# VectorE writes low parts one chunk further ahead beside the output gates of an HGRN2 layer

## The chip, the core and the metric

The kernel runs on 1 core of one Trainium2 chip. A time is the device time of one execution in microseconds (us). Three runs of the kernel before took 1814.8, 1816.38 and 1819.74 us; the median is 1816.38. The engines are named as in the profile: PE is TensorE (PEld its loads of weights), DVE is VectorE, ACT is ScalarE, SP is SyncE, which only issues DMAs. GpSimd computes nothing here.

## The reference, cut to what matters

One layer of depth 1 on 256 latent and 256 context tokens, width 2048. The mixer is HGRN2, a gated linear recurrence in two directions with 16 heads of 128 channels:

```
m_lat = split(silu(c) @ w_ada + b_ada, 6)            # shift, scale, gate, twice
a     = rms_norm(h) * (1 + scale) + shift            # latent and context
q, v, g = split(a @ w_in)                            # 2048 columns each
z     = clip(a @ w_f[d]), d = forward, backward
f     = lb + (1 - lb) * sigmoid(z);  k = 1 - f;  q = silu(q)
S_t   = diag(f_t) S_(t-1) + k_t v_t^T;   o_t = S_t^T q_t      # both directions, per head
y     = (rms_norm(o) * silu(g)) @ w_o                # g: the output gates
h     = h + gate1 * y
h     = h + gate2 * swiglu(modulated rms_norm(h));   out = rms_norm(h)
```

All products are in float32 precision.

## The kernel before, in words

**Weights in two parts.** A weight chunk is 128 x 1024 numbers. It lands in one of 7 buffers `raw`. ScalarE rounds it to `whi` (3 buffers, L510, function `hi`), VectorE subtracts that from the raw chunk and writes the rest, the low part, over the raw chunk (`rawlo`, L842, function `lo`). TensorE then computes three products for each tile: high by high, high by low, low by high. So each chunk passes ScalarE, VectorE and TensorE, in that order. `lo` waits for `s_hi` of its own chunk; TensorE waits for `s_lo` at the start of a chunk; `hi` of a chunk waits until TensorE has used up the chunk three before it.

**Positions.** Every engine walks one list, `positions()`, with one weight chunk per position. Chunks 0 to 127 give queries, values and forget gates of eight pairs of heads. Chunks 128 to 159 give the output gates (kind "G"); this text calls them g0 to g31, and their positions too. Then come the output projection, the gate and up projections of the FFN and the down projection.

**Scan steps.** Beside the matmuls of a position every engine works on a list of scan steps (j, n): step j of 14 of head n. Beside the output gates these are the steps of the last four heads, 12 to 15, by `tasks_tail`. On VectorE step 0 makes cumulated gates (L1035 to L1046), 1 and 2 the exponents of seven levels (L986, L987), 3 and 4 multiply the levels (L1005, L1006), 5 the operands of the state (L1057 to L1063), 7 and 9 place scores (L1013, L1017), 8 a state (L1079), 13 the normed output (L1085). Steps 6, 10, 11 and 12 have nothing on VectorE. On ScalarE step 2 is L648, step 3 L651, step 4 L634 to L645, step 7 L655, step 8 L659, step 11 L663, step 12 L668 and L670. On TensorE step 6 turns the operands (L1540) and step 11 sums squares (L1576).

**What VectorE does in a position**, in its order: `lo` of the chunk of the next position; clipping of the gates of the last pair (L950, in g0) and their logs and keys (L961, L963, L970, in g2 to g6); an output gate's product (L1093, in g11, g19 and g27); the scan steps of the list; and then a block of the adaLN weights, multiplied by silu(c) and added up (L934, L937, function `ada`), in g1, g4 to g18 and g20.

**What ScalarE does in a position**: `hi` of the chunk of the next position; exponents and logs of the last pair's gates (L594 to L597, g1 to g4); the SiLU of a unit of output gates with two loads of its table (L679, L681, in g10, g18 and g26); the scan steps; and the sigmoid (L604) that belongs to the logs. Each engine takes its instructions strictly in the program's order.

**Loads.** SyncE fills the seven `raw` buffers in the ring's order, in which weight chunks and adaLN blocks alternate here. A buffer is free again when TensorE has used the chunk (`s_used`) or VectorE has added the block (`s_ac`).

Of the kernel before, what the change touches and what calls it, by code (L numbers as in the profile page):

```python
# [64 lines left out]
def mod_blocks(ck):  # L65

    return list(range(FIRST + 4 * ck, min(FIRST + 4 * ck + 4, 64)))


C_G = C_B + GROUPS * BODY  # L70
C_WO = C_G + 4 * 8
# [15 lines left out]
def tasks_at(p, groups=True):  # L87

    return [(p - s, off) for s, off in head_slots() if 0 <= p - s <= 13]


def tasks_tail(p):

    out = []
    for s, head, stretched in ((-11, HEADS - 4, False), (-3, HEADS - 3, False), (5, HEADS - 2, True), (14, HEADS - 1, True)):
        for j in range(14):
            at = s + (6 * j) // 5 if stretched else s + j
            if at == p:
                out.append((j, head))
    return out  # L100


def positions():


    for g in range(GROUPS):
        for p in range(BODY):
            tasks = [(j, 4 * g + off) for j, off in tasks_at(p) if 4 * g + off >= 0]
            if g == 0 and p < 16:
                yield C_B + p, ("VQ", "Z")[p % 2], 0, p // 2, tasks  # L110
            else:
                yield C_B + g * BODY + p, "Z" if p % 16 >= 8 else "VQ", 2 * g + p // 16, p % 8, tasks
    for p in range(32):
        yield C_G + p, "G", p // 8, p % 8, tasks_tail(p)


def build(nc, x, c, ctx, c_ctx, w_ada, b_ada, norm_mix, norm_ffn, lb_logits, w_in, w_f, o_norm, w_o,
# [13 lines left out]
    with stack:  # L131
        at = {}
# [324 lines left out]
        def low(ck):  # L457

            return rawlo[:, SEQ["w", ck] % RAW, :]
# [15 lines left out]
        def ada_sum(e):  # L475

            return bank[3] if e < 6 else mx
# [361 lines left out]
        def _(dve):  # L839
            def lo(ck):  # L840
                dve.wait_ge(s_hi, ck + 1)
                dve.tensor_tensor(low(ck), raw[:, SEQ["w", ck] % RAW, :], whi[:, ck % SPL, :].bitcast(F32),  # L842
                                  ALU.subtract).then_inc(s_lo, 1)
# [9 lines left out]
            def mod_lo(n):  # L853
                if mod_direct(n):
                    return
                j = SPLIT_MOD.index(n)
                dve.wait_ge(s_mh, j + 1)
                dve.tensor_tensor(dlow[n % MRAW][:, :], dslot[n % MRAW], mhi[j % MHI][:, :].bitcast(F32),
                                  ALU.subtract).then_inc(s_ml, 1)

            def modulation(e):


                dve.wait_ge(s_at, e + 1)
                b = bias[:, 2 * e:2 * e + 2]
                nm = vec[:, R_NMIX + 2 * e:R_NMIX + 2 * e + 2]
                each_b = bass.AP(tensor=b.tensor, offset=b.offset, ap=[list(b.ap[0]), [KD, 2], [1, 2], [0, 2]])
                each_nm = bass.AP(tensor=nm.tensor, offset=nm.offset, ap=[list(nm.ap[0]), [1, 2], [0, 2]])
                turned = mod_bank(e)[:, 0:16].rearrange("p (m k i s) -> p m k i s", m=2, k=2, i=2)
                v = modx[:, 2 * e:2 * e + 2, :, :].rearrange("p k m i -> p m k i")  # L870
                dve.tensor_tensor(v, turned[:, :, :, :, 0], each_b, ALU.add).then_inc(s_md, 1)
                dve.wait_ge(s_md, 3 * e + 1)
                dve.tensor_tensor(v, turned[:, :, :, :, 1], v, ALU.add).then_inc(s_md, 1)
                dve.wait_ge(s_md, 3 * e + 2)
                dve.scalar_tensor_tensor(out=scl[:, 2 * e:2 * e + 2, :], in0=modx[:, 2 * e:2 * e + 2, 1, :], scalar=1.0,
                                         in1=each_nm, op0=ALU.add, op1=ALU.mult).then_inc(s_md, 1)

            def a_lo(k):
                dve.wait_ge(s_ah, k + 1)
                dve.tensor_tensor(alo[:, k, :], xn[:, k, :], ahi[:, k, :].bitcast(F32), ALU.subtract).then_inc(s_al, 1)  # L880

            def x_norm(k):
                dve.tensor_tensor(xn[:, k, :], xT[:, k, :], rstd[:, :], ALU.mult).then_inc(s_xn, 1)
# [58 lines left out]
            def clip_gates(pr):  # L942
                if pr >= 2:
                    dve.wait_ge(s_cum, 2 * pr - 2)
                for i, (d, h) in enumerate(UNITS):
                    if i < 3:
                        dve.wait_ge(s_zd, 3 * pr + i + 1)
                    else:
                        dve.wait_ge(s_used, C_B + 16 * (pr + 1))
                    dve.tensor_scalar(gates[pr % 2][:, h, d, :], z_out(pr, 2 * d + h), -CLIP, CLIP, ALU.max,  # L950
                                      ALU.min).then_inc(s_zc, 1)

            def log_gates(pr, i):

                d, h = UNITS[i]
                b = pr % 2
                n = 4 * pr + i
                G, K = gates[b][:, h, d, :], keyq[b][:, h, 2 * d, :]
                dve.wait_ge(s_ze, 3 * n + 3)
                dve.wait_ge(s_zc, n + 1)  # L960
                dve.tensor_tensor(K, G, zt[:, i % 2, 0, :], ALU.add).then_inc(s_zy, 1)  # L961
                dve.wait_ge(s_zy, 2 * n + 1)
                dve.tensor_tensor(G, zt[:, i % 2, 1, :], zt[:, i % 2, 0, :], ALU.subtract).then_inc(s_zy, 1)  # L963

            def keys(pr, i):
                d, h = UNITS[i]
                K = keyq[pr % 2][:, h, 2 * d, :]
                dve.wait_ge(s_mod, 1)
                dve.wait_ge(s_zk, 4 * pr + i + 1)
                dve.tensor_scalar(K, K, oml[:, 2 * pr + h:2 * pr + h + 1], None, ALU.mult).then_inc(s_k, 1)  # L970

            def scale_queries(pr):
                dve.wait_ge(s_qev, pr + 1)
                Q = keyq[pr % 2][:, :, 1, T:TT]
                dve.tensor_scalar(Q, Q, QSCALE, None, ALU.mult).then_inc(s_qs, 1)
# [112 lines left out]
            def gate_outputs(u):  # L1088
                for i in range(2):
                    dve.wait_ge(s_gev, 2 * u + i + 1)  # L1090
                    dve.wait_ge(s_on, 4 * u + 2 * i + 2)
                    v = oT[:, 4 * u + 2 * i:4 * u + 2 * i + 2, :]
                    dve.tensor_tensor(v, v, zt[:, i, 0, :].rearrange("p (k t) -> p k t", k=2), ALU.mult).then_inc(s_y, 1)  # L1093

            def add_modulation(e):
# [3 lines left out]
                o = 2 * KD + 8 * e  # L1099
                dve.tensor_tensor(v, ada_sum(e)[:, 0:8], bias[:, o:o + 8], ALU.add).then_inc(s_av, 1)  # L1100

            for ck, kind, u, r, tasks in positions():
                if u == 0 and kind == "VQ":
                    for n in mod_blocks(ck):
                        mod_lo(n)
                    if r < 5:
                        x_norm(6 + 2 * r)
                        x_norm(7 + 2 * r)
                if u == 0 and kind == "Z" and r < 7:
                    for n in mod_blocks(ck)[:3]:  # L1110
                        mod_lo(n)
                    modulation(r + 1)
                    a_lo(2 * r + 2)
                    a_lo(2 * r + 3)
                    for n in mod_blocks(ck)[3:]:
                        mod_lo(n)
                lo(ck + 1)
                p = (ck - C_B) % 16
                if p == 0 and C_B + 16 <= ck <= C_G:
                    clip_gates((ck - C_B) // 16 - 1)  # L1120
                if ck == C_B + 16:
                    scale_queries(0)
                if kind == "Z" and r == 1 and u:
                    scale_queries(u)
                if 2 <= p < 7 and C_B + 16 <= ck < C_G + 7:
                    pr = (ck - C_B) // 16 - 1
                    if p <= 5:
                        log_gates(pr, p - 2)
                    if p >= 3:
                        keys(pr, p - 3)  # L1130
                if kind == "G" and r == 3 and u:
                    gate_outputs(u - 1)
                for e in ada_ends(ck - 1):
                    add_modulation(e)
                for j, n in tasks:
                    scan(j, n)
                for i in ada_blocks(ck):
                    ada(i)

# [66 lines left out]
            for u in range(2 * FG):  # L1206
                for r in range(8):
                    ck = C_FF + 8 * u + r
# [451 lines left out]
def ada_blocks(ck):  # L1660
    return [i for i in range(PADA) if ada_chunk(i) == ck]
# [14 lines left out]
def ada_ends(ck):  # L1676

    return [e for e in range(PADA // KD) if ada_chunk(KD * e + KD - 1) + 2 == ck]
# [43 lines left out]
```

## Time and profile before

| what | value |
|---|---|
| median of three runs | 1816.38 us |
| the profiled execution | 1817.04 us |
| its span, first to last instruction | 1815.3 us |
| busy over the span: PE, DVE, ACT | 97%, 71%, 50% |
| mean granted TensorE clock, as a share | 0.994 |
| DMA over the span | 353.84 MB, mean 195 GB/s |

The chain that ended last is PE for 86% and DVE for 9% of the span. Busy shares are means over stages that have different limits; the output gates take only about 140 of the 1815 us, from about 832 to 972 us after the start.

### The profile page before, as it was taken

What the parts mean: (1) busy time and instruction counts of PE and PEld (TensorE: products, weight loads), DVE (VectorE), ACT (ScalarE), POOL (GpSimd) and SP (SyncE); (2) the same over time, 40 slices, a digit from 0 to 9 for tenths busy, and PEclk for the clock granted to TensorE, in tenths of its full rate; (3) what the DMA queues carried; (4) which work ended last, traced back from release to release, by engine and by line L of the source; (5) the groups of instructions that cost most, each with busy time, mean ns of one, the idle gap of its engine ahead of it and who ended that gap; (6) DMA issues with size and microseconds to landing.
All of it is one profiled execution on the core that took longest, in us unless ns stands there. A gap on an engine that the chain in (4) does not pass through costs nothing.

```text
span 1815.3 us, 25245 instructions
## 1 busy us (share of the span) xinstructions
PE 1764.5 (97%) x9791; PEld 1503.9 (83%) x9791; DVE 1284.5 (71%) x1999; ACT 915.4 (50%) x1297; POOL 0.2 (0%) x4
## 2 busy tenths in 40 slices
PE   7999999999999999999889989999999999999997
PEld 3667989898989898988789878888888888888886
DVE  5876979796979796979985575555555555555755
ACT  5776635353645454545455554444444444445544
POOL 0000000000000000000000000000000000000000
PEclk9999999999999999999999999999999999999999
DMA  8987745554444554445657556777767777666553
GB/s 292 300 276 240 220 152 151 153 167 134 152 140 143 153 179 130 151 138 142 216 193 263 186 152 212 229 231 224 227 215 237 222 227 227 218 195 195 190 195 128
DMA packets 203737, 353.84 MB, mean 195 GB/s; under 512 B 17953, under 2 KB 116578, under 8 KB 202594
## 3 DMA queue, kind: packets, MB, share of 16 engines
q1 hardware_dynamic: 203426, 352.18, 61.8%
q8 instruction: 77, 1.26, 0.3%
q14 instruction: 42, 0.34, 0.1%
q10 hardware_dynamic: 192, 0.05, 0.0%
HBM read 350.06 MB, written 2.11 MB: 194 GB/s over the span
## 4 chain that ended last, share of the span: by engine, by line
PE 86%; DVE 9%; issue 2%; ACT 2%; DMA 1%; ACTq 0%; SPq 0%; DVEq 0%
PE bank L1476 9%; PE bank L1478 9%; PE bank L1477 9%; PE bank L1342 7%; PE bank L1343 7%; PE bank L1344 7%; PE bank L1359 3%; PE bank L1360 3%; PE bank L1361 3%; PE bank L1496 3%; PE bank L1497 3%; PE bank L1498 3%; PE score L1558 2%; PE score L1496 1%; PE score L1497 1%
## 5 line engine op out<-in xcount | busy, mean ns | idle before, releaser
L842 DVE TENSOR_TENSOR rawlo<-raw,whi 128x1024 fp32r<-128x1024 f32 x456 | 556.4, 1223 | 378.5 <-ACT whi L510 377.8
L510 ACT ACTIVATE whi<-raw 128x1024 fp32r<-128x1024 f32 x456 | 481.1, 1058 | 596.2 <-PE bank L1478 240.6
L1342 PE MATMUL bank<-ahi,whi 128*128 128x256 f32 (+1 forms) x976 | 333.4, 342 | 10.7 <-DVE rawlo L842 10.5
L1343 PE MATMUL bank<-alo,whi 128*128 128x256 f32 (+1 forms) x976 | 325.8, 334 | 0.0
L1344 PE MATMUL bank<-ahi,rawlo 128*128 128x256 f32 (+1 forms) x976 | 325.7, 334 | 0.0
L1476 PE MATMUL bank<-whi,ahi 128*128 128x512 f32 x704 | 275.9, 392 | 1.8 <-DVE alo L1188 1.8
L1478 PE MATMUL bank<-whi,alo 128*128 128x512 f32 x704 | 274.6, 390 | 0.0
L1477 PE MATMUL bank<-rawlo,ahi 128*128 128x512 f32 x704 | 274.5, 390 | 0.0
L1342 PEld LDWEIGHTS bank<-ahi,whi 128*128 128x128 f32 x976 | 185.4, 190 | 31.7 <-DVE rawlo L842 10.2
L1344 PEld LDWEIGHTS bank<-ahi,rawlo 128*128 128x128 f32 x976 | 185.2, 190 | 18.4
L1343 PEld LDWEIGHTS bank<-alo,whi 128*128 128x128 f32 x976 | 185.5, 190 | 17.3
L1476 PEld LDWEIGHTS bank<-whi,ahi 128*128 128x128 f32 x704 | 132.6, 188 | 29.3 <-issue 2.2
L1478 PEld LDWEIGHTS bank<-whi,alo 128*128 128x128 f32 x704 | 132.5, 188 | 27.8
L1477 PEld LDWEIGHTS bank<-rawlo,ahi 128*128 128x128 f32 x704 | 132.6, 188 | 27.2
L937 DVE SCALAR_TENSOR_TENSOR aacc<-raw,cs,aacc 128x1024 f32<-128x1024 f32 x120 | 153.3, 1277 | 0.5
L1359 PE MATMUL bank<-whi,ahi 128*128 128x256 f32 x512 | 148.1, 289 | 1.2 <-DVE arena L950 1.2
L1361 PE MATMUL bank<-whi,alo 128*128 128x256 f32 x512 | 144.7, 283 | 0.0
L1360 PE MATMUL bank<-rawlo,ahi 128*128 128x256 f32 x512 | 144.7, 283 | 0.0
L1359 PEld LDWEIGHTS bank<-whi,ahi 128*128 128x128 f32 x512 | 98.0, 191 | 4.8 <-DVE rawlo L842 2.4
L1360 PEld LDWEIGHTS bank<-rawlo,ahi 128*128 128x128 f32 x512 | 97.9, 191 | 0.8
L1361 PEld LDWEIGHTS bank<-whi,alo 128*128 128x128 f32 x512 | 97.8, 191 | 0.0
L1496 PE MATMUL bank<-whi,ahi 128*128 128x512 f32 x240 | 93.6, 390 | 1.0 <-DVE rawlo L842 1.0
(233 smaller groups left out, 2487.8 us busy)
## 6 DMA issues: line engine op xcount, KB each, us to landing
raw<-in_w_ada_dram SPq DMA_DIRECT2D x128, 512.0 KB, 4.1
raw<-in_ffn_w_gate_dram SPq DMA_DIRECT2D x88, 512.0 KB, 3.7
raw<-in_ffn_w_up_dram SPq DMA_DIRECT2D x88, 512.0 KB, 3.7
raw<-in_ffn_w_down_dram SPq DMA_DIRECT2D x88, 512.0 KB, 4.5
raw<-in_hg_w_in_dram SPq DMA_DIRECT2D x128, 256.0 KB, 4.0
raw<-in_hg_w_f_dram SPq DMA_DIRECT2D x128, 256.0 KB, 4.0
work<-in_w_ada_dram SPq DMA_DIRECT2D x66, 256.0 KB, 5.2
raw<-in_hg_w_in_dram SPq DMA_DIRECT2D x32, 512.0 KB, 4.8
```

What stands on the lines that cost most here:

```text
L510: act.activation(whi[:, ck % SPL, :], raw[:, q % RAW, :], ACT.Copy).then_inc(s_hi, 1)
L842: dve.tensor_tensor(low(ck), raw[:, SEQ["w", ck] % RAW, :], whi[:, ck % SPL, :].bitcast(F32), ALU.subtract).then_inc(s_lo, 1)
L1342: pe.matmul(dst, w, ah, start=start, stop=False, skip_group_check=True)
L1343: pe.matmul(dst, w, al, start=False, stop=False, skip_group_check=True)
L1344: return pe.matmul(dst, wl, ah, start=False, stop=stop, skip_group_check=True)
L1359: pe.matmul(dst, ahi[:, k, tk], whi[:, s, o], start=st, stop=False, skip_group_check=True)
L1360: pe.matmul(dst, ahi[:, k, tk], low(ck)[:, o], start=False, stop=False, skip_group_check=True)
L1361: last = pe.matmul(dst, alo[:, k, tk], whi[:, s, o], start=False, stop=end, skip_group_check=True)
L1476: pe.matmul(dst, ahi[:, k, tk], whi[:, s, o], start=first, stop=False)
L1477: pe.matmul(dst, ahi[:, k, tk], low(ck)[:, o], start=False, stop=False)
L1478: last = pe.matmul(dst, alo[:, k, tk], whi[:, s, o], start=False, stop=end)
L1496: pe.matmul(dst, ahi[:, slot, tk], whi[:, s, o], start=start, stop=False)
```

## The change

In the position of an output gate chunk whose list of scan steps and adaLN blocks holds two things or more, VectorE writes, behind its first scan step, the low part of the chunk after the next (`lo(ck + 2)`). The next position then leaves its own `lo` out. The rule holds in g0 to g2, g4 to g18 and g20, 19 of the 32 positions. The number of instructions is the same. TensorE's, ScalarE's and SyncE's instructions are the same and in the same order; only VectorE's order changes.

```
+            early = set()
             for ck, kind, u, r, tasks in positions():
...
-                lo(ck + 1)
+                if ck not in early:
+                    lo(ck + 1)
...
-                for j, n in tasks:
+                ahead = kind == "G" and C_G <= ck < C_WO - 1 and len(tasks) + len(ada_blocks(ck)) >= 2
+                for at, (j, n) in enumerate(tasks):
                     scan(j, n)
+                    if ahead and at == 0:
+                        lo(ck + 2)
+                        early.add(ck + 1)
                 for i in ada_blocks(ck):
                     ada(i)
```

VectorE in g1 before. The first row is the low part of g2, the row before last that of g3; between them lie step 4 of head 13 and an adaLN block (L937); the last row begins g2:

```order
L842 TENSOR_TENSOR rawlo<-raw,whi 128x1024
L1005 TENSOR_TENSOR work<-work,arena 128x2x16x8
L1006 TENSOR_TENSOR work<-work,arena 128x2x16x8
L1005 TENSOR_TENSOR work<-work,arena 128x2x32x4
L1006 TENSOR_TENSOR work<-work,arena 128x2x32x4
L1005 TENSOR_TENSOR work<-work,arena 128x2x64x2
L1006 TENSOR_TENSOR work<-work,arena 128x2x64x2
L1005 TENSOR_TENSOR work<-work,arena 128x2x128
L1006 TENSOR_TENSOR work<-work,arena 128x2x128
L937 SCALAR_TENSOR_TENSOR aacc<-raw,cs,aacc 128x1024
L842 TENSOR_TENSOR rawlo<-raw,whi 128x1024
L961 TENSOR_TENSOR arena<-arena,zt 128x512
```

The same position now. The first row is here the low part of g3, since g2's stands in g0 already, ahead of step 3 of head 13:

```order
L842 TENSOR_TENSOR rawlo<-raw,whi 128x1024
L1005 TENSOR_TENSOR work<-work,arena 128x2x16x8
L1006 TENSOR_TENSOR work<-work,arena 128x2x16x8
L1005 TENSOR_TENSOR work<-work,arena 128x2x32x4
L1006 TENSOR_TENSOR work<-work,arena 128x2x32x4
L1005 TENSOR_TENSOR work<-work,arena 128x2x64x2
L1006 TENSOR_TENSOR work<-work,arena 128x2x64x2
L1005 TENSOR_TENSOR work<-work,arena 128x2x128
L1006 TENSOR_TENSOR work<-work,arena 128x2x128
L937 SCALAR_TENSOR_TENSOR aacc<-raw,cs,aacc 128x1024
L961 TENSOR_TENSOR arena<-arena,zt 128x512
L963 TENSOR_TENSOR arena<-zt 128x512
```

The low part of g3 has moved ahead of step 4 of head 13 and of the adaLN block.

VectorE at the end of g5 and in g6, the difference (minus: before, plus: now). The first row is g5's adaLN block. The low part is that of g7 where it is taken away and that of g8 where it is put in; L1013 and L1017 are step 9 of head 13, the L986 and L987 behind them step 1 of head 14:

```order
 L937 SCALAR_TENSOR_TENSOR aacc<-raw,cs,aacc 128x1024
-L842 TENSOR_TENSOR rawlo<-raw,whi 128x1024
-L970 TENSOR_SCALAR arena<-arena,oml 128x512
-L1013 TENSOR_TENSOR work<-score,ident 128x128
-L1017 COPY_PREDICATED work<-masks,score 128x128 x7
+L970 TENSOR_SCALAR arena<-arena,oml 128x512
+L1013 TENSOR_TENSOR work<-score,ident 128x128
+L1017 COPY_PREDICATED work<-masks,score 128x128 x7
+L842 TENSOR_TENSOR rawlo<-raw,whi 128x1024
 L986 TENSOR_TENSOR work<-work 128x2x2x64
 L987 TENSOR_TENSOR work<-work 128x2x2x64
```

In g7 the list is step 10 of head 13, step 2 of head 14 and a block; step 10 has nothing on VectorE, so the low part of g9 stands right behind g6's block, where that of g8 stood, and the rows there read alike.

VectorE from the end of g18 to g20, the difference. The low part taken away is that of g19; L1093 is the product of an output gate in g19, then follow the low part of g21, L1085 (step 13 of head 14) and L1057 (step 5 of head 15) in g20:

```order
 L1006 TENSOR_TENSOR work<-work,arena 128x2x128
 L937 SCALAR_TENSOR_TENSOR aacc<-raw,cs,aacc 128x1024
-L842 TENSOR_TENSOR rawlo<-raw,whi 128x1024
 L1093 TENSOR_TENSOR work<-work,zt 128x512 x2
 L842 TENSOR_TENSOR rawlo<-raw,whi 128x1024
 L1085 SCALAR_TENSOR_TENSOR work<-ob,vec,rstd 128x256
+L842 TENSOR_TENSOR rawlo<-raw,whi 128x1024
 L1057 TENSOR_TENSOR work<-work,arena 128x384
```

The low part taken away there is that of g20, which now stands in g18; the one put in is that of g22, ahead of step 5 of head 15. That of g21 keeps its place.

## Rows read from the trace of the kernel before

**Rows 1.** The page: busy us, share and instructions of each engine
```profile
PE 1764.5 (97%) x9791; PEld 1503.9 (83%) x9791; DVE 1284.5 (71%) x1999; ACT 915.4 (50%) x1297; POOL 0.2 (0%) x4
```

**Rows 2.** Windows: length, busy us per engine (instructions), granted clock, DMA share, GB/s
```profile
830.00:925.00 95.00, 78.32 (x613) 75.28 (x612) 93.07 (x178) 55.35 (x87) 0.00 (x0) 0.98 0.62 202
941.00:1040.00 99.00, 99.00 (x572) 87.44 (x572) 55.52 (x73) 52.28 (x72) 0.00 (x0) 1.00 0.65 218
```

**Rows 3.** Waits of PE and DVE, 830 to 925: total us, times, longest
```profile
PE bank L1342 <- DVE rawlo L842: 10.5, 7, 3.7
DVE rawlo L842 <- ACT whi L510: 0.5, 1, 0.5
```

**Rows 4.** Timeline of DVE, g0 to g2: start, us, idle before in brackets
```profile
834.72 0.41 DVE L1005 TENSOR_TENSOR work<-work,arena 128x256 f32<-128x256 f32 x1
...
836.72 1.22 DVE L842 TENSOR_TENSOR rawlo<-raw,whi 128x1024 fp32r<-128x1024 f32 x1
...
840.55 1.27 DVE L937 SCALAR_TENSOR_TENSOR aacc<-raw,cs,aacc 128x1024 f32<-128x1024 f32 x1
841.74 1.21 DVE L842 TENSOR_TENSOR rawlo<-raw,whi 128x1024 fp32r<-128x1024 f32 x1
842.88 0.68 DVE L961 TENSOR_TENSOR arena<-arena,zt 128x512 f32<-128x512 f32 x1
...
844.20 0.48 DVE L1085 SCALAR_TENSOR_TENSOR work<-ob,vec,rstd 128x256 f32<-128x256 f32 x1
```

**Rows 5.** Timeline of ACT, the end of g1, and g2
```profile
839.88 1.04 ACT L510 ACTIVATE whi<-raw 128x1024 fp32r<-128x1024 f32 x1
...
843.59 0.63 ACT L604 ACTIVATE arena<-arena 128x512 f32<-128x512 f32 x1 [0.87 <-DVE arena L961]
844.13 1.04 ACT L510 ACTIVATE whi<-raw 128x1024 fp32r<-128x1024 f32 x1
```

**Rows 6.** Timeline of DVE, behind step 1 and step 2 of head 14
```profile
869.66 1.28 DVE L937 SCALAR_TENSOR_TENSOR aacc<-raw,cs,aacc 128x1024 f32<-128x1024 f32 x1
...
874.68 1.27 DVE L937 SCALAR_TENSOR_TENSOR aacc<-raw,cs,aacc 128x1024 f32<-128x1024 f32 x1
875.87 1.22 DVE L842 TENSOR_TENSOR rawlo<-raw,whi 128x1024 fp32r<-128x1024 f32 x1
```

**Rows 7.** Timeline of ACT, g7 and g8
```profile
869.78 1.49 ACT L648 ACTIVATE work<-work 128x1536 f32<-128x1536 f32 x1 [7.45 <-DVE work L987]
871.17 1.04 ACT L510 ACTIVATE whi<-raw 128x1024 fp32r<-128x1024 f32 x1
...
876.61 1.04 ACT L510 ACTIVATE whi<-raw 128x1024 fp32r<-128x1024 f32 x1
```

**Rows 8.** Timeline of DVE, g16 to g20
```profile
917.06 1.28 DVE L937 SCALAR_TENSOR_TENSOR aacc<-raw,cs,aacc 128x1024 f32<-128x1024 f32 x1
...
927.75 1.23 DVE L842 TENSOR_TENSOR rawlo<-raw,whi 128x1024 fp32r<-128x1024 f32 x1
```

**Rows 9.** Timeline of ACT, g17 and g18
```profile
918.99 1.04 ACT L510 ACTIVATE whi<-raw 128x1024 fp32r<-128x1024 f32 x1
920.05 1.28 ACT L679 ACT_TABLE_LOAD   x1
...
926.67 1.05 ACT L510 ACTIVATE whi<-raw 128x1024 fp32r<-128x1024 f32 x1
```

**Rows 10.** Timeline of DVE in g20 (step 5 of head 15), and of PE
```profile
932.63 0.75 DVE L1063 TENSOR_TENSOR work<-work,arena 128x256 f32<-128x256 f32 x2
933.44 0.55 PE L1540 MATMUL mx<-ident,work 128*128 128x128 f32 x3
```

**Rows 11.** Windows around the one fall of the clock in this stage
```profile
910.00:915.00 5.00, 1.32 (x11) 1.12 (x11) 4.98 (x10) 2.43 (x2) 0.00 (x0) 1.00 0.88 295
915.00:920.00 5.00, 5.00 (x32) 5.00 (x31) 5.00 (x11) 2.83 (x2) 0.00 (x0) 0.66 0.26 95
```

## The prediction

> **What bounds the kernel now.** I read the page's busy table first. Over the whole span TensorE is busy 97% and VectorE 71% [rows 1], so a change of VectorE's order is worth something only in a stretch where VectorE is the late one. The windows show where that is. From 830 to 925 us VectorE is busy 93.07 of 95 us and TensorE only 78.32; from 941 to 1040 us TensorE is busy all 99.00 us and VectorE 55.52 [rows 2]. The change acts in g0 to g20, from about 832 to 935 us, so nearly all of it lies in the first kind of stretch. The waits of that stretch come next: TensorE waits 10.5 us in seven pauses for low parts, while VectorE waits 0.5 us in all for a high part [rows 3]. VectorE's order of work is then the path. TensorE's pauses there are a result of VectorE's length, not a store of time that an order can give back, and any new pause of VectorE is paid in full. Last I laid the timelines of VectorE and ScalarE beside each other, position by position.
>
> **What the change does to VectorE's length.** It removes nothing and adds nothing: 19 subtractions go forward past work that stays. Their own cost is the same. What is new is their wait. The low part of the chunk after the next needs that chunk's high part, which ScalarE makes only behind all scan steps and gate work of the present position. Before, VectorE asked for a high part that ScalarE had written a position earlier, and so it waited 0.5 us in 95 [rows 3]. Now it asks about one position earlier. Behind the waiting subtraction stand the rest of the scan steps and the adaLN block, in order, and SyncE's next load waits for the block's buffer. So I compare for each moved low part when VectorE gets to it and when the high part is there. Prices from start to start: a low part 1.14 us (842.88 - 841.74), three levels' multiplications 2.00 (836.72 - 834.72), four levels' 2.69 (840.55 - 837.86, where 837.86 = 836.72 + 1.14), the block 1.20 (841.74 - 840.55 = 1.19), the logs of a gate 1.32 (844.20 - 842.88) [rows 4].
>
> Low part of g3, in g1. Step 12 leaves nothing on VectorE, so the subtraction stands right behind step 3 of head 13. VectorE gets there at 834.72 + 1.14 + 2.00 = 837.86. ScalarE's high part begins at 839.88 and ends at 840.92 [rows 5]; ScalarE is busy with gate exponents and step 4, none of which comes sooner. Pause 3.06.
>
> Low part of g4, in g2. VectorE goes on at 840.92 and gets there at + 1.14 + 2.69 + 1.20 + 1.32 + 0.40 (L1085) = 847.67. ScalarE's sigmoid starts 0.71 behind L961 (843.59 - 842.88) and the high part is done 1.58 later (844.13 + 1.04 - 843.59) [rows 4, 5]. L961 starts at 845.95, so it is there at 848.24. Pause 0.57.
>
> Low parts of g5 to g7 have the same logs and sigmoids. That of g5 keeps its place and its pause of 0.5; for g7 I take 0.2 new.
>
> Low part of g9, in g7. Step 10 leaves nothing on VectorE. It gets there at 869.66 + 1.20 = 870.86 (there g8's subtraction stood) [rows 6]. ScalarE has the long exponentials of step 2 first, which start when VectorE's levels end, and then the high part from 871.17 to 872.21 [rows 7]. Pause 1.35.
>
> Low part of g10, in g8. The same with step 3: VectorE at 875.87 [rows 6], the high part from 876.61 to 877.65 [rows 7]. Pause 1.78.
>
> g10 to g16: from here ScalarE has little, since VectorE is late already and most positions give it one short step. I count 0.
>
> Low part of g19, in g17. Reckoned from the end of step 2 of head 15 at 917.06 [rows 8], VectorE now has g18's low part and the block first: 917.06 + 1.14 + 1.20 = 919.40. The high part runs from 918.99 to 920.03 [rows 9]. Pause 0.63.
>
> Low part of g20, in g18. Step 11 leaves nothing on VectorE. It gets there at 920.03 + 1.14 + 2.00 + 1.20 = 924.37. ScalarE has two table loads around the SiLU from 920.05, steps 11 and 4, and then the high part from 926.67 to 927.72 [rows 9]. Before, VectorE took that chunk at 927.75, just behind it [rows 8]. Pause 3.35.
>
> The pauses add to 3.06 + 0.57 + 0.2 + 1.35 + 1.78 + 0.63 + 3.35 = 10.9 us. Low parts g21 and later that keep their place are late by as much.
>
> The handover. In g20 the subtraction of g22 now stands ahead of step 5 of head 15, another 1.14 us. TensorE turns the result of that step (L1540) at 933.44, and VectorE's L1063 ends at 932.63 + 0.75 = 933.38 [rows 10]: TensorE has 0.06 us of room. So TensorE gets past this point 10.9 + 1.14 - 0.06 = 12.0 us later. Behind it TensorE is busy without a gap [rows 2] and nothing is given back. The whole delay goes to the end.
>
> Sum, against the profiled execution's 1817.04 us: 1817.04 + 12.0 = 1829.0. That execution is 0.66 above the median of 1816.38, so against the median 1828.4.
>
> **A rule weighed.** VectorE starts its instructions in order in every row I read, and the pause in front of a subtraction holds back what is behind it. The Trainium skill, page "TensorE: Matmul & The Clock Gate", section "Architectural detail: the array is 16× 32×32, not 1× 128×128", says that ScalarE and VectorE have strict first-in first-out queues while TensorE may pull weight loads forward. By that rule the pauses cost what I reckon; if the waiting subtraction could be passed by the multiplications behind it, the 10.9 would be near 0. No row before shows a pass, so the trace agrees.
>
> **Bounds of the unknown.** Each pause is the distance of two rows, right if ScalarE's chain keeps its place against VectorE's. If TensorE, late with steps 10 and 11, holds ScalarE up (L663 needs its sums), they grow; the largest pause of TensorE so far is 3.7 us [rows 3], and I allow one such, + 4. If the smaller pauses (0.57, 0.2, 0.63) vanish and those of g9 and g10 halve, 3.0 goes. Nothing here can be below zero but the handover, where the gain rival sits. Own range of the forecast: 1825 to 1833.
>
> **Rivals.**
>
> Nothing moves. VectorE's sum is unchanged and the pauses are taken up because VectorE would have waited anyway. For it: the low part alone needs no new work. Against it: VectorE has only 95 - 93.07 = 1.9 us free in the stretch [rows 2]. Time 1816.4.
>
> Only the first pause stays. If ScalarE, which is busy only 55.35 of 95 us [rows 2], runs further ahead than I think once VectorE is 3 us late, later pauses shrink: 3.06 + 0.57 + 1.14 = 4.8. Time 1821.2. Against it: ScalarE's steps 2 and 3 start on VectorE's own ends, so they shift with VectorE [rows 7].
>
> Faster. TensorE's seven waits for low parts vanish since each low part is there a position sooner; 10.5 us at most, 1805.9. It decides if high parts are ready when asked for. It needs VectorE to have room, which it has not; a partial version gives the one large wait of 3.7 [rows 3], at 1812.7.
>
> More than reckoned: the clock. TensorE was busy 1.32 us of 910 to 915, and in the next 5 us its granted clock was 0.66 on the mean, that is some 3.4 us at the lower of its levels, 1.2 GHz; it cost nothing since TensorE then waited anyway [rows 11]. With longer pauses of TensorE there will be two to four such falls. One that meets TensorE where it is the late engine costs half of 3.4, 1.7 us, and then delays high parts through used chunks. With two of them and the 4 us above it is 1828.4 + 7 = 1835. The Trainium skill, the same page, section "What's actually happening", has it that the throttled clock is the default and activity releases it. By that rule too the longer pauses bring more falls, and the trace agrees with the one it shows.
>
> **How the numbers follow.** Forecast 0.73, more than reckoned 0.06, only the first pause 0.09, nothing 0.08, faster 0.04. A measurement here can tell about 0.3%, 5.4 us, from no change. Slower by more: 0.73 + 0.06 and about half of the 0.09, 0.84. Within: the other half and most of nothing, 0.12. Faster: 0.04. The range 1821.5 to 1833 takes in the forecast's own range and reaches down to the case of one pause.
>
> **What the changed profile would show.** VectorE's waits for L510 in the stretch of the output gates rise from 0.5 to about 11 us, with pauses near 3 us in front of the low parts of g3 and g20, and 1.3 and 1.8 in front of g9 and g10. TensorE waits longer for L1063 of head 15, and its unbroken stretch begins some 12 us later. Everything behind it, from the output projection on, is the old timeline shifted by 12. Wrong would be a VectorE without pauses there (then high parts come earlier than I read), or an unbroken stretch of TensorE that starts as early as before although VectorE paused.

## The result, and the profile after

The changed kernel took 1832.21 us (median of 4 runs, 1828.53 to 1835.57), the kernel before beside it 1817.1 us (median of 4, 1814.8 to 1819.74). The ratio is 1.0082, with a 95% interval of 1.007 to 1.0094: slower by about 15 us. The profiled execution took 1828.53 us, with a span of 1826.7 us, 11.5 us above the one of before.

The page of after, busy us and share of each engine (answers to [rows 1]):

```profile
PE 1765.0 (97%) x9791; PEld 1505.2 (82%) x9791; DVE 1285.3 (70%) x1999; ACT 915.6 (50%) x1297; POOL 0.2 (0%) x4
```

Nothing was added to any engine: the counts are the same and no engine is more than 0.8 us busier, apart from weight loads with 1.3. All but a few tenths of the 11.5 us is waiting. The next fence has the waits of the kernel after from 825 to 945 us (engine, line, tile, who is waited for: total us, times, longest). L1348 is L1342 of before, six lines are added above it; in the same way L1546 is L1540, L1582 is L1576, L1594 is L1588.

```profile
PE bank L1348 <- DVE rawlo L842: 11.4, 6, 2.8
DVE rawlo L842 <- ACT whi L510: 11.2, 8, 3.2
PE mx L1546 <- DVE work L1063: 11.0, 3, 7.1
...
PE mx L1582 <- ACT rstd L663: 4.4, 2, 2.9
```

One row of the same list of the kernel before, for the third of these:

```profile
PE mx L1540 <- DVE work L1063: 2.7, 2, 1.7
```

Against [rows 3], VectorE's wait for high parts went from 0.5 us to 11.2, and TensorE's wait for low parts stayed (10.5 to 11.4): the earlier low parts did not spare TensorE anything. (The windows differ a little. From 825 to 945 us VectorE waits 2.5 us in the kernel before, but the 2.0 more are the wait in front of g25's low part, which is as long in both and falls behind the window in the kernel after.) TensorE's wait for the operands that it turns in step 6 of a head (L1546) grew from 2.7 us to 11.0, up to 7.1 us at a time, since the scan step that makes them stands behind the waiting subtraction in VectorE's order.

The timeline of VectorE in the kernel after, only the rows from g1 to g20 with a pause of 0.3 us or more in front (start, us, what, idle before in brackets, and who ended it):

```profile
839.00 1.23 DVE L842 TENSOR_TENSOR rawlo<-raw,whi 128x1024 fp32r<-128x1024 f32 x1 [2.97 <-ACT whi L510]
846.35 1.23 DVE L842 TENSOR_TENSOR rawlo<-raw,whi 128x1024 fp32r<-128x1024 f32 x1 [0.52 <-ACT whi L510]
851.50 1.22 DVE L842 TENSOR_TENSOR rawlo<-raw,whi 128x1024 fp32r<-128x1024 f32 x1 [0.52 <-ACT whi L510]
855.21 0.17 DVE L1100 TENSOR_TENSOR mod<-bank,bias 128x8 f32<-128x8 f32 x1 [0.76 <-PE bank L1594]
876.13 1.23 DVE L842 TENSOR_TENSOR rawlo<-raw,whi 128x1024 fp32r<-128x1024 f32 x1 [1.30 <-ACT whi L510]
882.96 1.23 DVE L842 TENSOR_TENSOR rawlo<-raw,whi 128x1024 fp32r<-128x1024 f32 x1 [1.73 <-ACT whi L510]
908.66 1.22 DVE L842 TENSOR_TENSOR rawlo<-raw,whi 128x1024 fp32r<-128x1024 f32 x1 [0.31 <-ACT whi L510]
926.58 1.23 DVE L842 TENSOR_TENSOR rawlo<-raw,whi 128x1024 fp32r<-128x1024 f32 x1 [0.59 <-ACT whi L510]
934.25 1.23 DVE L842 TENSOR_TENSOR rawlo<-raw,whi 128x1024 fp32r<-128x1024 f32 x1 [3.24 <-ACT whi L510]
```

The subtractions are those of g3, g4, g5, g9, g10, g16, g19 and g20. The one of g5 paused as long before. The new pauses for high parts are 2.97 + 0.52 + 1.30 + 1.73 + 0.31 + 0.59 + 3.24 = 10.66 us. (Two more, of 0.12 and 0.13 us in front of g2's and g15's, are left out.)

A pause as shown is a little shorter than the delay that it makes. A subtraction is shown with 1.22 us, but the next instruction starts 1.14 us behind its start where nothing holds it up [rows 4]; where VectorE pauses, that overlap is lost. So I also took the row behind each moved low part and compared its start with that of the same row before, with 1.14 us for each low part that stands ahead of it in one kernel only. Across the pauses the lateness grows by 3.05 us (g3), 0.61 (g4), 1.39 (g9), 1.82 (g10), 0.39 (g16), 0.68 (g19) and 3.33 (g20), 11.27 in all, and by 0.85 at L1100.

Windows of the kernel after, over the stretch bound by VectorE and over the one behind it (length, busy us per engine with instructions, granted clock, DMA share, GB/s; they answer to [rows 2]):

```profile
830.00:937.00 107.00, 82.62 (x633) 79.93 (x632) 93.52 (x179) 57.84 (x96) 0.00 (x0) 0.92 0.55 173
953.00:1052.00 99.00, 99.00 (x570) 87.36 (x570) 55.63 (x74) 52.84 (x73) 0.00 (x0) 1.00 0.62 215
```

The first window is 12 us longer than that of before for the same work of VectorE (93.52 us to 93.07), and the second shows TensorE without a gap again: nothing is given back there. The timeline of TensorE has the handover, where it turns the operands that step 5 of head 15 makes, at 933.44 us before [rows 10], and now:

```profile
944.95 0.55 PE L1546 MATMUL mx<-ident,work 128*128 128x128 f32 x3 [1.50 <-DVE work L1063]
```

That is 11.5 us later, the whole difference of the two executions. This execution reached g0 1.9 us sooner than the one of before, ahead of anything that the change moves, so the stage itself costs 13.4 us (13.45 by the unrounded starts).

### The profile page after: what moved, and what is told of

The parts are those of the page before. It is cut to its first block, busy times and chain, and to the rows that moved or that the text cites. A ratio compares the mean times of both kernels' runs of the same rounds, so it can differ in the third digit from the quotient of the medians.

```text
span 1826.7 us, 25247 instructions
## 1 busy us (share of the span) xinstructions
PE 1765.0 (97%) x9791; PEld 1505.2 (82%) x9791; DVE 1285.3 (70%) x1999; ACT 915.6 (50%) x1297; POOL 0.2 (0%) x4
## 4 chain that ended last, share of the span: by engine, by line
PE 85%; DVE 9%; issue 2%; ACT 2%; DMA 1%; SPq 0%; ACTq 0%; DVEq 0%
PE bank L1482 9%; PE bank L1484 9%; PE bank L1483 9%; PE bank L1348 7%; PE bank L1349 7%; PE bank L1350 7%; PE bank L1365 3%; PE bank L1366 3%; PE bank L1367 3%; PE bank L1502 3%; PE bank L1503 3%; PE bank L1504 3%; PE score L1564 3%; PE score L1502 1%; PE score L1504 1%
## 5 line engine op out<-in xcount | busy, mean ns | idle before, releaser
L1348 PE MATMUL bank<-ahi,whi 128*128 128x256 f32 (+1 forms) x976 | 334.3, 343 | 11.6 <-DVE rawlo L842 11.4
L1348 PEld LDWEIGHTS bank<-ahi,whi 128*128 128x128 f32 x976 | 186.3, 191 | 32.3 <-DVE rawlo L842 12.6
L937 DVE SCALAR_TENSOR_TENSOR aacc<-raw,cs,aacc 128x1024 f32<-128x1024 f32 x120 | 153.3, 1278 | 0.4
```

Source lines behind the costliest of these rows:

```text
L1348: pe.matmul(dst, w, ah, start=start, stop=False, skip_group_check=True)
```

## The experiments

Each time is a median of runs on the same chip as runs of the kernel before, and a ratio is against these. Those of before were 1816.27 us in the first set (13 runs: the next four experiments), 1818.08 in the second (19: the filled gaps, the moves without a pause, the shorter sums) and 1817.34 in the third (15: the rest).

**The changed kernel again.** No edit.

> The changed kernel once more, unchanged, on the chip that the three others of this call use. Theory (VectorE pauses for high parts that ScalarE has not made yet; the stage is VectorE's, so each pause goes to the end): 12 to 15 us over the kernel before, and the profile shows the pauses at the same low parts again, 3.0 before g3's, 1.3 and 1.7 before g9's and g10's, 0.6 and 3.2 before g19's and g20's. Rival (most of the distance is TensorE's clock, which fell in other places in the execution profiled): the pauses are the same but the executions spread by 5 us or more with the mean clock, 0.991 for the faster and 0.986 for the slower.

Measured 1834.81 us (1828.97 to 1835.97, 4 runs), ratio 1.0101 [1.0086, 1.0116]. The profiled execution was the 1828.97 one. Its pauses in front of g4, g9, g10, g19 and g20 are those of the kernel after, 0.52, 1.30, 1.73, 0.59 and 3.25 us, and L1100 paused 0.97. The one of g3 was 2.48 us, not 2.97, behind one of 1.27 in front of the low part of g1, which the change does not move. The other executions took 1833.8, 1835.82 and 1835.97. So the kernel after has executions near 1829 and others near 1834 to 1836. The rival of the expectation, that the executions spread by 5 us or more with the mean granted clock, came true beside the theory: over both sets the three executions of 1828.5 to 1829.8 us have a mean clock of 0.991, the one of 1833.8 has 0.989, and the four of 1834.6 to 1836 have 0.986 or 0.987. No profile caught one of 1834 to 1836.

**Only the first pause.** The move is made in g0 and g1 alone:

```
-                ahead = kind == "G" and C_G <= ck < C_WO - 1 and len(tasks) + len(ada_blocks(ck)) >= 2
+                ahead = kind == "G" and ck - C_G in (0, 1)
```

> Only g0 and g1 write a low part ahead, so that one new pause is left, that before the low part of g3; the handover at g20 is as before. Theory of the pauses: 3.0 us over the kernel before, VectorE waits 3.0 us once before g3's low part and is late by 3.0 all the way to g21. Rival that the slack of ScalarE takes such a pause back later: under 1 us. Rival that the order itself (low parts ahead of scan steps) is what costs, in proportion to the 19 places: 2 of 19 of the cost, 1.4 us.

Measured 1820.53 us (1818.96 to 1823.4, 7 runs), ratio 1.0024 [1.0013, 1.0034]. VectorE's pauses in the profile:

```profile
832.15 1.23 DVE L842 TENSOR_TENSOR rawlo<-raw,whi 128x1024 fp32r<-128x1024 f32 x1 [1.64 <-ACT whi L510]
841.39 1.23 DVE L842 TENSOR_TENSOR rawlo<-raw,whi 128x1024 fp32r<-128x1024 f32 x1 [2.47 <-ACT whi L510]
```

The second is that of g3 (2.97 in after). The first is in front of the low part of g1, which the change does not move, and the kernel with VectorE's old order further down shows 1.27 us there too (0.10 in before, 0.00 in after, 1.27 in the repeat). Why it differs from one execution to the next isn't known; where it is over 1 us, g3 waits some 0.5 less. Against the kernel before, VectorE is 0.97 us late at g1 and 3.7 late from g7 on, and it stays at 3.7 within 0.1 to g23: the pause of g3 is paid in full and not made up over the positions behind it. Another 1.3 us came between g23 and g25, where the clock had fallen twice shortly before (at 919 and 929 us). So of the 5.6 us that this execution lost between g0 and g25, some 2.6 came at g3, 1.5 at g1 and 1.3 at the last place. The median is 4.3 over the kernel before where I had expected 3.0; how the other executions divide isn't known.

**High parts sooner too.** VectorE's order of after, and ScalarE writes the high part ahead of its scan steps at the places where VectorE asks early (all later lines are 5 higher here):

```
+            hi_early = set()
...
-                hi(ck + 1)
+                if ck not in hi_early:
+                    hi(ck + 1)
...
+                if kind == "G" and ck - C_G in (1, 2, 7, 8, 17, 18):
+                    hi(ck + 2)
+                    hi_early.add(ck + 1)
                 for j, n in tasks:
                     scan(j, n)
```

> VectorE keeps the whole changed order. ScalarE writes the high part of the chunk after the next ahead of its scan steps too, in g1, g2, g7, g8, g17 and g18, where the pauses were; its gate exponents and the SiLU keep their places. Theory of the pauses: VectorE's waits for high parts fall from 11 to about 2 us, and the kernel is 2 to 4 us over the kernel before, 1.1 of it the handover. Rival that the order of low parts ahead of scan steps costs by itself (scan steps late on VectorE hold up TensorE): still 8 to 13 us over it.

Measured 1823.46 us (1821.34 to 1824.63, 5 runs), ratio 1.0034 [1.0022, 1.0046]: 11 us below the median of the kernel after in the same set, with VectorE's order unchanged. The profiles differ less: from g0 to g25 the repeat loses 14.1 us and this kernel 6.2, so 7.9 us are gone. Three of the four executions of the kernel after in that set were of the longer kind and none of these five is, which would make the medians differ by more. Its waits from 825 to 945 us:

```profile
PE bank L1353 <- DVE rawlo L847: 7.8, 4, 2.6
PE mx L1551 <- DVE work L1068: 6.4, 3, 3.7
...
DVE rawlo L847 <- ACT whi L510: 4.9, 6, 1.8
```

VectorE's wait for high parts fell to 4.9 us, from 11.2 in after and 11.7 in the repeat. So most of the cost is not VectorE's order by itself, but that the order asks for something ScalarE has further back in its queue. Some 6 to 7 us above the kernel before remain, more than the 2 to 4 that I had expected. The profiled execution loses 6.2 us between g0 and 944.72 us of the kernel before (g25's low part). Three of the pauses left are in front of the low parts of g11 (0.87), g16 (1.82) and g22 (1.21), and the same 1.1 us comes at the handover as in after. By the rows behind them these make 0.96, 1.92, 1.30 and 1.15 us, 5.3 of the 6.2. Which of these would go with a still earlier high part I did not try.

**High parts sooner alone.** The same six places on ScalarE, with VectorE's order of before.

> VectorE's order is that of the kernel before; ScalarE alone writes the high part of the chunk after the next ahead of its scan steps in g1, g2, g7, g8, g17 and g18. Theory: VectorE did not wait for these high parts before, so the time is that of the kernel before within 1 us. Rival that the earlier high parts delay ScalarE's scan steps, which would explain a part of what the early-high kernel has over the kernel before: 2 to 3 us slower.

Measured 1817.4 us (1815.55 to 1820.12, 11 runs), ratio 0.9999 [0.999, 1.0008]. Sooner high parts are worth nothing where nobody asks for them sooner, so what they took off the changed kernel they took off its pauses.

**Without the move in g20.** The low part of g22 stays behind step 5 of head 15; the 18 other moves stand.

```
+                ahead = kind == "G" and ck - C_G in (0, 1, 2, 4, 5, 6, 7, 8, 9, 10, 11, 12, 13, 14, 15, 16, 17, 18)
```

> The changed kernel without its last place: g20 no longer writes the low part of g22 ahead of step 5 of head 15. Theory: all pauses stay, the handover goes; 1.1 us under the changed kernel, and TensorE passes L1063's reader of head 15 that much earlier. Rival (TensorE is then held by the low part of g21 anyway): the same time as the changed kernel.

Measured 1829.63 us (1829.05 to 1835.93, 6 runs), ratio 1.0076 [1.0062, 1.009]. By medians that can't be told from the other two runs of the kernel after, since one us is less than its executions differ, and only one of its six was of the longer kind (1835.93). The timelines tell it. Against the kernel before, the low part of g21 starts 10.38 us late in after and 10.69 in the repeat, and that of g25, behind the handover (944.72 us before), 11.51 and 11.84: a step of 1.13 and 1.15. In this kernel both are at 11.70 or 11.71. TensorE's own row, the turn at 933.44 us before, has the same step: its lateness is above that of g21's low part by 1.13 or 1.14 us in after, the repeat, the filled kernel and the two more executions further down, and by 0.00 in this one. (The one-pause kernel and that with only the moves without a pause have 1.4 and 2.1 us there without the move. TensorE does not wait at the turn in these but is itself late, with its clock at the lower level from 919 to 923 and 929 to 932 us in the one and from 919 to 929 in the other.) In the kernel after the row of g25 stands at 956.23 us; in this kernel:

```profile
956.43 1.23 DVE L842 TENSOR_TENSOR rawlo<-raw,whi 128x1024 fp32r<-128x1024 f32 x1 [2.01 <-ACT whi L510]
```

**Only the moves without a pause.** Ahead in g0, g4 to g6 and g9 to g16, that is without all those whose low part paused for 0.5 us or more, and without g20:

```
+                ahead = kind == "G" and ck - C_G in (0, 4, 5, 6, 9, 10, 11, 12, 13, 14, 15, 16)
```

> The change kept only where the high part was there in time: g0, g4 to g6 and g9 to g16, 12 of 19 places; not in g1, g2, g7, g8, g17, g18 and g20. Theory of the pauses: VectorE waits about 1 us for one high part (g11's, which the two table loads hold up), and the kernel is 0 to 2 us over the kernel before. Rival that the moved order costs by itself: 12 of 19 of the 12 to 15 us, 8 us.

Measured 1819.61 us (1817.92 to 1821.54, 11 runs), ratio 1.0007 [0.9999, 1.0016]. Twelve low parts written about a position sooner gain nothing. VectorE waited 3.2 us for high parts, where I had expected about 1; 1.65 of it was for g16. TensorE still waited 7.3 us for low parts. Its profiled execution lost 5.0 us between g0 and the row at 944.72 of before, 2.1 of it between g23 and g25 (see above) and 1.7 at g16, but it had begun the stage 2.8 us sooner. So these moves harm little where they don't pause, and there was no gain in them to begin with: in this stretch TensorE waits for the sum of VectorE's work, not for the place of a subtraction in it. The rival that each moved subtraction costs by itself, 8 us for twelve, is refuted.

**TensorE's gaps filled.** The kernel after, with needless matmuls (their results are overwritten) in three long gaps: 48 in g3 ahead of the turn of operands that waits 7.1 us, 18 ahead of g18 and 20 ahead of step 11 of head 14. The first of them (the two others are loops of the same form, without the added wait):

```
+                    if n == 13:
+                        pe.wait_ge(s_zc, 4 * PAIRS)
+                        for _ in range(48):
+                            pe.matmul(bank[2][:, 0:T], ahi[:, 0, T:T + P], ahi[:, 1, T:TT], start=True, stop=True, skip_group_check=True)
```

> The changed kernel with needless matmuls in three of TensorE's waits: 48 in g3 ahead of the turn of head 13's operands, 18 ahead of g18's start and 20 ahead of step 11 of head 14, all into banks that are free there. VectorE's and ScalarE's work is untouched. Theory that the pauses of VectorE make up 12 to 13 us and TensorE's half clock the rest: the pauses stay (3.0, 1.3, 1.7, 0.6, 3.2), the clock stays full in g3 to g5 and from g17 to g19, the 1 us for which VectorE waits for the sums of the adaLN group in g4 goes, and the executions at 1834 to 1836 us become rare or none; median about 1828. Rival that these falls of the clock cost nothing because TensorE waits anyway: same times as the changed kernel, 1829 to 1836, or later by the needless work.

Measured 1831.01 us (1829.61 to 1833.11, 5 runs), ratio 1.0064 [1.005, 1.0078]. In the kernel after the granted clock fell in the first gap (at 845 us) and in the second (at 924), and was still at the lower level in the third. A window of after over the first:

```profile
847.00:850.00 3.00, 0.69 (x3) 0.69 (x4) 2.96 (x8) 1.23 (x3) 0.00 (x0) 0.50 0.04 15
```

The same window of the filled kernel:

```profile
847.00:850.00 3.00, 2.86 (x24) 2.66 (x23) 2.48 (x6) 2.54 (x4) 0.00 (x0) 1.00 0.44 162
```

The clock held at its upper level of 2.4 GHz there (0.50 in the row of after is the lower one, 1.2 GHz), and VectorE's pause at L1100 was gone. From 929 to 932 us it was at 1.00 too, where after has 0.50. But VectorE's waits for high parts were 12.7 us, g16's now 1.62, and the clock fell elsewhere, at 884.5, 894.8 and 942.6 us: over the 120 us from 830 to 950 the mean granted clock is 0.93 in both profiles. The fall at 942.6 met TensorE where it is the late engine, right at the handover. VectorE then waited for TensorE's scores 1.2 us longer than in after (0.49 there):

```profile
950.81 0.29 DVE L1013 TENSOR_TENSOR work<-score,ident 128x128 f32<-128x128 f32 x1 [1.69 <-PE score L1571]
```

None of its five executions was above 1833.11, where three of the kernel after's four in the first set were at 1833.8 or more; with so few, that hints at the clock as what parts the two kinds and doesn't show it. Since the profiled execution had as much of the lower clock in the stage as that of after, it can't say how much of the loss is the clock's. Two others can: with a mean clock of 0.995 over the whole execution they took 1829.61 and 1831.01 us, and the kernel before of the same set at 0.995 took 1816.11. So most of the loss, 13 us or more, stands in executions with no more of the lower clock than the kernel before can have. Where it fell in these isn't known.

**The kernel after twice more.** No edit, one profiled execution each.

> The changed kernel once more, one execution with its profile. If it is one of those at 1834 to 1836: theory of the clock, that the half-clock stretches are more or stand where TensorE is the late engine (around 920 to 945), and the VectorE shift there is 4 to 6 us larger than in the profiles at 1829. Rival: the added time stands before g0, where nothing was changed.

> One more execution of the changed kernel with its profile, for the same question as e_look2: where the executions at 1834 to 1836 us spend what they have over those at 1829.

They took 1832.6 us and 1828.95 us. The second looks like the profile of after. The first reached g0 1.33 us later than after did, ahead of the change. It paused 1.78 us at L1100 (0.76 in after) and 1.66 in front of the low part of g16 (0.31 in after). Where the latter comes from is to be seen in a window of that execution:

```profile
897.00:904.00 7.00, 5.41 (x28) 5.12 (x27) 7.00 (x12) 2.04 (x3) 0.00 (x0) 0.52 0.53 200
```

and in the same window of after:

```profile
897.00:904.00 7.00, 5.87 (x51) 5.88 (x52) 6.86 (x13) 2.49 (x4) 0.00 (x0) 1.00 0.28 82
```

With the clock at 0.52 TensorE got 28 matmuls done where it had done 51. SyncE loads the next chunk into a buffer that TensorE has finished with, and did so at 906.18 us, not 902.25. The high part waited for that chunk, as ScalarE's timeline of that execution has it:

```profile
911.30 1.06 ACT L510 ACTIVATE whi<-raw 128x1024 fp32r<-128x1024 f32 x1 [1.95 <-DMA raw<-in_hg_w_in_dram]
```

and VectorE, the late engine, paused for the high part. At 944.72 us of the kernel before, this execution is 15.26 us late and after 11.51; of the 3.75 us between them 1.33 were there at g0, 1.02 came at L1100 and 1.35 at g16. So a third of it stood ahead of g0, as the rival of the expectation had it, and the rest in the stage. Stretches of TensorE at the lower clock, where it is not the late engine, do reach VectorE, through a load. The other profiles with this move fit: g16 paused 1.62 to 1.82 us in four of them (this one, the filled kernel, sooner high parts, only the moves without a pause), in all of which the clock fell between 890 and 897 us, and 0.31, 0.02 and 0.23 us in after, the repeat and the other execution of this pair, where it was at the upper level from 891 to 910 us. Without the move in g20 it paused 0.45 us, though the clock fell at 895.1 us for 3.4 us, so it counts where in the program the clock falls.

**Shorter sums, the kernel before otherwise.** What would help in this stretch is less work of VectorE, by the experiments above. The adaLN sums end at positions given by a list; with earlier ends their blocks (L937) stand in the projections ahead, where TensorE is the late engine. TensorE's wait ahead of the sixth sum then has the form of those ahead of the first five (the first edit below):

```
-                if e < 5:
+                if e < 6 and ADA_ENDS[e] < C_G + 8:
...
-ADA_ENDS = (34, 54, 82, 102, 131, 150)
+ADA_ENDS = (34, 50, 66, 86, 102, 129)
```

> Not the change but the kernel before with less work for VectorE in the stage: the sixteen adaLN blocks of the last group before the FFN's, 1.2 us each on VectorE, stand beside the forget gates and values (the groups end at positions 34, 50, 66, 86, 102 and 129 in place of 34, 54, 82, 102, 131 and 150). Theory that the stage is bound by VectorE's length: TensorE's waits for low parts in g0 to g20 shrink from 10.5 to about 3, and the kernel is 3 to 6 us under the kernel before; not the full 19, since TensorE has only some 16 us of waits there and the earlier positions become fuller. Rival that the order of low parts is what holds TensorE: no gain.

Measured 1814.14 us (1811.3 to 1816.81, 9 runs), ratio 0.9976 [0.9966, 0.9987]: it beats both kernels. The ratio is against the kernel before; the medians differ by 3.9 us. Blocks between 830 and 945 us went from 17 to 1. Its window answers to the first of [rows 2]:

```profile
830.00:925.00 95.00, 85.10 (x649) 80.76 (x648) 84.52 (x185) 58.14 (x93) 0.00 (x0) 0.99 0.45 133
```

TensorE is busy 85.10 of 95 us and no longer 78.32, and its wait for low parts from 825 to 950 us is 3.4 us, not the 10.5 of [rows 3]. From 600 to 830 us it stays busy 228.01 of 230 us (229.39 before), but the blocks are not free ahead of the gates: in this profile g0's low part comes 6.9 us later than before, and g25's 2.0 us sooner. The stretch between them got 8.9 us shorter and what stands ahead of it 6.9 longer. VectorE now waits 9.6 us for high parts from 825 to 950 us, so in a part of the stretch it is no longer the late engine. About 19 us of VectorE's work were moved out for a gain of some 4.

## Why the prediction was right

The mechanism is what the runs show; that the median lies inside the range is in part luck. The range ended at 1833. The ten executions of the unedited changed kernel have a median of 1833.2, and the repeat's four have 1834.81.

**The path.** It held that VectorE's order is the path, that a pause of it is paid in full, and that no low part that comes sooner gives TensorE time. The one-pause kernel shows the second, the moves without a pause (1.0007) the third. "Nothing moves" and "faster" are both refuted by the interval of after, and "only the first pause" by its profile, since the others stayed as long as reckoned.

**The pauses.** Forecast and measured: g3 3.06 and 2.97; g4 0.57 and 0.52; g9 1.35 and 1.30; g10 1.78 and 1.73; g19 0.63 and 0.59; g20 3.35 and 3.24. Reading when the operand is ready, and when the engine gets to asking for it, off the old timelines gave each within 0.11 us of the idle time shown. The forecast was of delays from start to start, though, and against these it is closer still: 3.05, 0.61, 1.39, 1.82, 0.68 and 3.33, each within 0.05. g7's 0.2 did not occur. The sum was 10.9; the six measure 10.88 as delays, and the idle time with g16's is 10.66. That these agree is the strongest sign that ScalarE's chain kept its place against VectorE's.

**What had been counted as nothing.** "g10 to g16: I count 0" failed by a little: the low part of g16 paused 0.31 us in one execution, 1.66 and 1.62 in others. ScalarE was idle there, as I had said; what was late was the chunk, and I had not followed it back through the loads to TensorE. And the pause of 0.76 at L1100 was not in the sum: VectorE adds the bias to a modulation there, and TensorE gave it late, having waited 7.14 us for the operands of step 6 of head 13 and then run at the lower clock. In delays, the six pauses make 10.88 us, g16 0.39, L1100 0.85 and the handover 1.13; of the 13.45 some 0.2 is left, in steps of about 0.1 that I can't name.

**The handover.** Forecast 1.14 - 0.06, measured 1.13 or 1.14 at TensorE's turn in five profiles of the whole moved order, and 0 without the move in g20.

**The sum.** 12.0 forecast; the stage cost 13.4, the execution ended 11.5 later as it had begun the stage 1.9 sooner. 1829.0 was forecast for the profiled execution and 1828.53 measured. That they are so close is in part luck: 1.4 too little in the stage against 1.9 that it did not know of.

**The clock.** The rival of more falls was given 0.06 and 1835 us. It is partly there. The median of 1832.21 lies 3.8 above the forecast, between the two, and the executions near 1834 to 1836 are at the rival's price. What I had mis-sized was not the price but how often: I took two such meetings to be rare, and about half of the executions end up there. The path that I had given it, through used chunks and high parts, is what the execution of 1832.6 us shows, with 1.35 us at g16, beside 1.02 at L1100. The direct price, 1.7 us where TensorE is the late engine, has three measurements at the handover: 1.2 in the filled kernel, and 1.4 and 2.1 in the one-pause kernel and that with only the moves without a pause. One reading was wrong: the fall in [rows 11] "cost nothing since TensorE then waited anyway", but the row has TensorE busy for all 5.00 us. It waited only behind it (2.17 us up to 924.17, for L663), which could take up what was lost. The Trainium skill, page "TensorE: Matmul & The Clock Gate", section "What's actually happening", has the throttled clock as the default that activity releases. Filling a gap with matmuls kept the clock in it at 1.00, so these traces agree.

**What stays open.** No execution of 1834 to 1836 us was profiled. Their mean granted clock is on record, 0.986 or 0.987 against 0.991, so that they have more of the lower clock is shown; where it stands, and that it is the cause of the 5 to 7 us and not a result of longer pauses, is argued. Why the low part of g1 pauses in some executions and not in others isn't known either.

## What to carry to other kernels

Where an engine is the late one because of the sum of its work, moving an instruction forward in its order gained nothing here, and cost whatever the moved instruction then waited for. So lay its new place against the time at which its producer has the operand ready, in that producer's own queue, and add the differences, from start to start. Moving consumer and producer together took away somewhat over half of the waits (11.7 to 4.9 us); moving work off the late engine is what gained. TensorE's longer idle stretches also brought more of the lower clock (a mean of 0.93 from 830 to 950 us in after), which sums of pauses leave out, so keep a margin above them.

## What the runs showed that I had not expected

- A delay of VectorE lasts: the one-pause kernel was 3.69 us late at g7 and 3.74 at g23, and made nothing good in between.
- TensorE at the lower clock in a stretch where it isn't the late engine cost VectorE 1.35 us (1.66 to 0.31), through a used chunk, a load 3.9 us later (906.18 to 902.25) and a high part.
- Filling three gaps with 86 matmuls kept the clock up in those and moved its falls to 884.5, 894.8 and 942.6 us, with the same mean clock over the stage (0.93) and a time within the range of the kernel without them. The last of these falls cost 1.2 us at the handover.
